# Cumulated gate columns taken at the end of the preceding step, rows from four transposes: a gated DeltaNet and sliding-window layer

## The reference

```python
beta = jax.nn.sigmoid(b)
g = -jnp.exp(a_log) * jax.nn.softplus(a + dt_bias)      # one value for each frame and head
G = jnp.cumsum(gc, axis=-1)                             # gc: g cut into chunks
decay = jnp.exp(jnp.where(causal, G[..., :, None] - G[..., None, :], -jnp.inf))
...
attn_intra = jnp.einsum('bhnid,bhnjd->bhnij', qc, kc) * decay
q_exp = qc * jnp.exp(G)[..., None]
k_tail = kc * jnp.exp(G[..., -1:] - G)[..., None]
g_last = jnp.exp(G[..., -1])
```

## Time and profile before

| what | value |
|---|---|
| median of 3 runs | 2282.87 us (2281.79 to 2283.89) |
| the profiled execution, its own time | 2285.99 us |
| its span in the trace | 2284.2 us |
| mean granted TensorE clock | 0.994 of full speed |
| TensorE busy | 2164.4 us, 95% of the span |
| VectorE busy | 1672.4 us, 73% |
| ScalarE busy | 782.7 us, 34% |
| GpSimd busy | 652.4 us, 29% |

### The profile page before, as it was taken

The page is one execution under the profiler, slowest core; times in us unless marked ns, Lnnn a source line. Parts: engine busy times, 40 slices in busy tenths (PEclk is TensorE's granted clock), DMA queues, the critical chain, the costliest instruction groups (busy, mean ns, idle before and its releaser), DMA issues.

```text
span 2284.2 us, 61174 instructions
## 1 busy us (share of the span) xinstructions
PE 2164.4 (95%) x25926; PEld 1858.0 (81%) x25926; DVE 1672.4 (73%) x4495; ACT 782.7 (34%) x2008; POOL 652.4 (29%) x875
## 2 busy tenths in 40 slices
PE   0389999999999999999999999999999999999996
PEld 0388888888888888888888888888888888888874
DVE  5887777777777777777777777777777777777764
ACT  0533333333333333333333333333333333333332
POOL 0022323322323332232333223233323233322322
PEclk9999999999999999999999999999999999999998
DMA  7100000000000000000000000000000000000000
GB/s 297 53 21 31 2 30 30 31 31 31 30 2 31 31 30 30 31 22 10 31 31 30 31 31 10 23 30 31 30 31 30 2 30 31 30 31 30 21 2 28
DMA packets 26321, 75.19 MB, mean 33 GB/s; under 512 B 5129, under 2 KB 9538, under 8 KB 25026
## 3 DMA queue, kind: packets, MB, share of 16 engines
q1 hardware_dynamic: 26050, 71.29, 8.9%
HBM read 54.50 MB, written 16.78 MB: 31 GB/s over the span
## 4 chain that ended last, share of the span: by engine, by line
PE 92%; DVE 4%; DMA 1%; ACT 1%; issue 0%; SPq 0%; POOLq 0%; POOL 0%; DVEq 0%; ACTq 0%
PE bank L402 37%; PE bank L594 14%; PE bank L409 11%; PE bank L417 9%; PE bank L432 4%; PE bank L452 3%; PE bank L436 2%; PE bank L562 1%; PE bank L528 1%; DVE w_raw L1204 1%; PE bank L549 1%; PE bank L380 1%; PE bank L471 1%; PE bank L440 1%; PE bank L457 1%; PE bank L444 1%
## 5 line engine op out<-in xcount | busy, mean ns | idle before, releaser
L402 PE MATMUL bank<-xt_half,w_raw 128*128 128x128 f16 x15360 | 933.6, 220 | 54.8 <-DVE w_raw L1204 54.3
L402 PEld LDWEIGHTS bank<-xt_half,w_raw 128*128 128x128 f16 x15360 | 896.4, 98 | 62.3 <-DVE w_raw L1204 54.5
L867 DVE SCALAR_TENSOR_TENSOR qkv<-conv_in,cols,qkv 128x128 f32<-128x128 f32 x1152 | 431.3, 416 | 3.5
L409 PE MATMUL bank<-w_raw,xt_half 128*128 128x264 f16 (+1 forms) x1536 | 283.0, 328 | 0.0
L1261 POOL TENSOR_TENSOR cw<-mt,small 128x256 f32<-128x256 f32 x160 | 114.7, 725 | 394.4 <-PE bank L432 373.3
L409 PEld LDWEIGHTS bank<-w_raw,xt_half 128*128 128x128 f16 x1536 | 147.9, 98 | 77.7 <-issue 5.3
L694 ACT ACTIVATE work<-bank 128x256 f32<-128x256 f32 x160 | 61.3, 383 | 397.8 <-PE bank L436 397.8
L594 PE MATMUL bank<-w_o,inv_t 128*128 128x512 f16 x768 | 171.0, 379 | 2.1 <-DVE inv_t L1140 2.1
L594 PE MATMUL bank<-w_o,out_b_half 128*128 128x512 f16 x768 | 171.0, 379 | 0.0
L659 ACT ACTIVATE tanh_c<-qkv 128x512 f32<-128x512 f32 x96 | 60.5, 630 | 270.2 <-DVE qkv L867 270.2
L594 PEld LDWEIGHTS bank<-w_o,inv_t 128*128 128x128 f16 x768 | 73.8, 98 | 85.5 <-DVE inv_t L1140 2.4
(11 more groups left out here) (219 smaller groups left out, 3765.6 us busy)
## 6 DMA issues: line engine op xcount, KB each, us to landing
x_in<-in_x_dram SPq DMA_DIRECT2D x32, 512.0 KB, 4.3
y_out<-in_x_dram SPq DMA_DIRECT2D x32, 512.0 KB, 4.0
out_dram<-y_out SPq DMA_DIRECT2D x32, 512.0 KB, 2.9
w_raw<-in_w_in_dram SPq DMA_DIRECT2D x8, 1024.0 KB, 12.2
w_o<-in_w_out_dram SPq DMA_DIRECT2D x8, 512.0 KB, 12.7
w_raw<-in_w_in_dram SPq DMA_DIRECT2D x8, 384.0 KB, 11.3
w_raw<-in_w_in_dram SPq DMA_DIRECT2D x8, 256.0 KB, 12.1
rot_tab<-in_rotary_dram SPq DMA_DIRECT2D x32, 64.0 KB, 3.9
```

Of the source, the lines that this page charges most:

```text
L402: last = mm(dst[:, 128 * b:128 * b + 128], w_half[:, c, ws, col:col + 128], xt_half[:, xs, c, :], start=(c == 0 and ws + xs == 0), stop=(c ...
L409: last = mm(dst[:, 0:n_col], xt_half[:, xs, c, :], w_half[:, c, ws, col:col + n_col], start=(c == 0 and ws + xs == 0), stop=(c == NC - 1 a ...
L867: last = v.scalar_tensor_tensor(dst, conv_in[:, b, i:i + TOK], tap, dst, ALU.mult, ALU.add)
```

## The change

TensorE gets a new function, `gate_columns`: one product of `upper` with `g_tok` (four columns) into bank 2. It is called at the end of the step in which `g_tok` was formed, between the transposes L608 and `fill(2)`, and waits for `g_ready` of tile t and `state_ready` of tile m. In step 0 it follows the last fill. The product L475 at the start of the step goes. The four row products L471 at the start of the step are replaced by four transposes of `g_cols`, broadcast, and these wait for `g_cols_used`. The wait for `out_a_ready`, which stood ahead of L475, stands ahead of the transposes of Q in place of `g_cols_used`.

VectorE copies the columns after `copy_xt` and ahead of the convolution of Q, instead of at the start of the next step. That copy waits for `g_col_t` and `exp_cols_ready`. At the start of the step the last column of the rows is still copied, now signalling `g_last_ready`.

```diff
+                def gate_columns():
+                    done(pe, g_ready, t)
+                    done(pe, state_ready, m)
+                    mm(bank[2][:, 0:4], upper, g_tok, start=True, stop=True).then_inc(g_col_t, 1)
+
                 if not mix:
                     fill(len(PIECES))
+                    gate_columns()
                     if prep:
                         turn_x(t + 1)
                     return
 
-                done(pe, g_ready, m)
-                done(pe, state_ready, m - 1)
+                done(pe, g_cols_used, m)
                 for h in range(4):
-                    last = mm(bank[2][:, 128 * h:128 * h + 128], g_tok[:, h:h + 1].broadcast_to([128, 128]),
-                              upper, start=True, stop=True)
+                    last = nc.tensor.transpose(heads(2)[:, h, :], g_cols[:, h:h + 1].broadcast_to([128, 128]), ident)
                 last.then_inc(g_row_t, 1)
-                done(pe, out_a_ready, m - 1)
-                mm(bank[3][:, 0:4], upper, g_tok, start=True, stop=True).then_inc(g_col_t, 1)
...
-                done(pe, g_cols_used, m)
+                done(pe, out_a_ready, m - 1)
                 for h in range(4):
                     last = nc.tensor.transpose(heads(3)[:, h, :], q4[:, h, :], ident)
...
                 last.then_inc(o_turned, 1)
+                if proj:
+                    gate_columns()
                 fill(2)
...
                     done(dve, g_row_t, m)
-                    done(dve, exp_cols_ready, m - 1)
-                    v.tensor_copy(g_cols[:, 8:12], heads(2)[:, :, TOK - 1])
-                    done(dve, g_col_t, m)
-                    v.tensor_copy(g_cols[:, 0:4], bank[3][:, 0:4]).then_inc(g_cols_used, 1)
-                    done(dve, g_cols_used, m)
+                    v.tensor_copy(g_cols[:, 8:12], heads(2)[:, :, TOK - 1]).then_inc(g_last_ready, 1)
+                    done(dve, g_last_ready, m)
                     v.tensor_tensor(g_cols[:, 4:8], g_cols[:, 8:12], g_cols[:, 0:4], ALU.subtract)
...
                 if prep:
                     copy_xt(t + 1, True)
                 if proj:
+                    done(dve, g_col_t, t)
+                    done(dve, exp_cols_ready, m)
+                    v.tensor_copy(g_cols[:, 0:4], bank[2][:, 0:4]).then_inc(g_cols_used, 1)
                     convolve(t, FILL_Q, range(4), qs_ready if mix else None, m)
```

More of the change, by code:

```diff
@@ L222, in build @@
             sem(n) for n in ("gram_t", "k_turned", "v_turned", "q_turned", "sq_ready"))
-        norm_link, k_norms_ready, norms_ready, key_norm_ready, m_ready, at_ready, vn_ready, k_tail_ready = (
-            sem(n) for n in ("norm_link", "k_norms_ready", "norms_ready", "key_norm_ready", "m_ready", "at_ready",
+        norm_link, g_last_ready, k_norms_ready, norms_ready, key_norm_ready, m_ready, at_ready, vn_ready, k_tail_ready = (
+            sem(n) for n in ("norm_link", "g_last_ready", "k_norms_ready", "norms_ready", "key_norm_ready", "m_ready", "at_ready",
                              "vn_ready", "k_tail_ready"))
```

## The result

The changed kernel takes 2268.44 us (median of 4 runs, 2267.31 to 2269.20), the kernel before 2283.38 us in the same comparison (median of 4, 2281.79 to 2285.98). The ratio is 0.9931, with a 95% interval of 0.9915 to 0.9946: faster by 0.7%, 14.9 us. The forecast was 15.6 us and 2267.3 us.

What follows compares the result with a forecast made beforehand. The prediction took gapless TensorE to bound the steady steps. It summed 13.4 us there, 2.3 in step 1 and -0.1 in the last step to 15.6 us, giving 2267.3 us, with an 8-in-10 range of 2263 to 2273 us.

Steps and rivals of the forecast that it cites:

- What bounds the kernel: Steady steps: TensorE is busy throughout at full clock, so work leaving its queue leaves the time if other engines keep up.
- Rows: Step's start: four transposes at 0.44 us replace products at 0.89 us, gaining 0.45 us a step, bounds 0.40 and 0.49.
- The column product: Moved between L608 and L402 at about the same cost: net 0, bounds -0.05 and +0.10 us a step.
- steady sum: Steps 2 to 31: thirty times 0.445 us gives 13.4 us gained, bounds 11.1 and 14.7.
- Slack: Gram products L417 behind the output's scaling (`y_used`): 0.16 us left of 0.80, with least favourable bounds 0.
- Rival A: Gram products wait for `y_used`, which takes the saving's place: 2270.6 to 2280.8 us, put at 2272; chance 0.14.
- Ends: First and last steps: 2.3 us gained and 0.1 us lost, with +-1.5 us for half-clock stretches in the last.
- step 1: First step: the wait at L495 goes and the fill behind starts earlier, gaining 2.3 us, bounds 0.5 and 2.8.
- last step's start: Saving swallowed by L417's wait for L1154; moved L475 delays the chain by 0.12 us.
- B: Ends go otherwise: a half-clock stretch more or first-step gain missing, 2269 to 2271 us; one less, 2265 to 2266; chance 0.10.
- C: Transposes in a row drop the clock to half at each step's start: 36 us slower in thirty, 2303 us; chance 0.02.
- D: Transposes of the broadcast column take two instructions like products, so only the first step gains: 2280.7 us; chance 0.02.

Runs made afterwards that it cites:

- transposes twice: Changed kernel with each of the four row transposes issued twice: 2283.38 us, ratio to the kernel before 0.9994.
- rows as products: Changed kernel with the four row transposes undone to products of the gate with the triangle: 2281.62 us, ratio to the kernel before 0.9991.
- before, conv. late: Kernel before with one unread VectorE reduction (0.60 us) added ahead of the convolution of Q: 2286.38 us, ratio 1.0005.
- changed, conv. late: Changed kernel with one unread VectorE reduction (0.60 us) added ahead of the convolution of Q: 2285.40 us, ratio to the kernel before 0.9990.
- copy first: Changed kernel with the copy of the columns ahead of the turned input's copy: 2267.81 us, ratio to the kernel before 0.9930.
- columns first: Changed kernel with the column product ahead of the transposes L611 (old L608): 2269.73 us, ratio to the kernel before 0.9941.
- transposes alone: Kernel before with rows from four transposes, columns still formed and copied at the step's start: 2285.88 us, ratio 1.0009.

## Why the prediction was right

*What bounds the kernel.* Right. TensorE had no gap before and has none after, and the same 0.44 us once more (the transposes twice) are found in full in the period.

*Rows.* Forecast 0.44 us for the four transposes and 0.45 us of gain; measured 0.44 us in the chain, and 0.45 us of gain by the run that undoes only this (13.6 us in thirty steps). Two instructions became one of the same length.

*The column product.* Forecast net 0, with -0.05 to +0.10. Measured: 0.12 us at its new place, 0.02 us on the fill behind it, and 0.05 us less on the transposes of K. A gain of 0.03 to 0.04 us a step, inside the bounds I had named and not taken. Thirty steps gained 14.8 us, where the forecast had 13.4 (bounds 11.1 and 14.7). The steady sum is the term that was mis-sized, by 1.4 us, mostly through this. Its bounds were also too narrow for its own terms: a gain of 0.40 to 0.49 us from the rows and a cost of -0.05 to +0.10 us from the column product make 0.30 to 0.54 us a step, 9.0 to 16.2 us in thirty, and only that range holds the 14.8.

*Slack.* Forecast 0.16 us left of 0.80, measured 0.09 by the timeline and 0.12 by the added reduction. TensorE's part before it had become 0.63 us shorter instead of 0.57, the chain 0.08 longer (10.15 us from the turned input to the signal against 10.07). Rival A was real in kind and did not come about for want of a tenth of a us; with 0.60 us of other work it took the whole gain.

*Ends.* The stages by the trace, in us: the columns are from the second half of L380 in step 0 to the first output projection; from there thirty steps and the first half of one more output projection (5.18 us); from there to the waiting L417 of the last step; and the rest of the span. With the columns first, the column product (0.14 us) lies in the second stage instead of the third.

| kernel | step 1 | thirty steps | last step's start | rest |
|---|---|---|---|---|
| before | 63.40 | 2018.58 | 13.14 | 56.80 |
| changed | 61.14 | 2003.78 | 13.29 | 55.73 |
| rows as products | 61.15 | 2017.37 | 13.28 | 60.52 |
| transposes twice | 61.14 | 2016.79 | 13.27 | 56.92 |
| before, conv. late | 62.37 | 2018.58 | 13.14 | 60.53 |
| changed, conv. late | 61.87 | 2018.33 | 13.28 | 58.79 |
| copy first | 61.17 | 2003.78 | 13.28 | 56.82 |
| columns first | 61.17 | 2004.91 | 13.18 | 55.77 |
| transposes alone | 68.72 | 2014.98 | 13.62 | 54.90 |

Step 1 gained 2.26 us (2.3 forecast) in this pair of executions, and by the mechanism that was forecast. This is the L380 from which the 63.40 us before are counted:

```profile
132.28 0.62 PE L380 MATMUL bank<-masks,shared 128*128 128x128 f16 x8 [0.69 <-DVE shared L826]
```

VectorE's line from L380 to the end of its product L1005 (now L1007) takes 22.97 us before and 22.96 after. The fill that needs this product started 25.36 us behind L380 before, 2.4 us late, and 23.11 us after. In all five kernels that form the columns early and add nothing ahead of VectorE's convolution this fill starts 23.11 to 23.13 us behind L380, though TensorE reaches the Gram products anywhere from 13.03 to 14.01 us. That is why step 1 takes 61.14 to 61.17 us in all five, and why products, double transposes and the earlier copy changed nothing there.

But the size of this gain was in part luck. Before the change the 48 matmuls behind the wait at L495 took 4.03 us, at a mean clock of 0.68. The prediction had them run at the full clock once that idle time was gone. In the kernel before with the added reduction the idle time is longer (2.87 us), and the clock was full all the same:

```profile
148.95 2.84 PE L402 MATMUL bank<-xt_half,w_raw 128*128 128x128 f16 x48
```

Its step 1 took 62.37 us, with more work on VectorE. Against such an execution of the kernel before, the gain of step 1 would have been 1.2 us at most. What decides which of the two comes is not shown by any run.

The last step's start lost 0.15 us (0.12 forecast). The rest is the same program in all, but took 54.9 to 60.5 us. It goes with the granted clock there; these are the busy times of that stage in the run with the rows as products and in the one with the transposes alone:

```profile
2223.80:2284.30 60.50, 40.80 (x248) 29.69 (x248) 25.43 (x57) 12.29 (x34) 14.20 (x15) 0.79 0.07 27
```

```profile
2230.30:2285.20 54.90, 35.13 (x248) 25.45 (x248) 25.46 (x57) 12.36 (x34) 14.20 (x15) 0.90 0.08 29
```

The same 248 matmuls took 40.8 us of TensorE at a mean clock of 0.79 and 35.1 us at 0.90. The forecast gave the ends +-1.5 us. That was too narrow for the last stage of a single execution (5.6 us between these), and it is the reason why the spans of two executions tell 18.7 us and the medians 14.9: 14.8 in thirty steps and 2.3 in step 1, less 0.15, are 16.9, and the setup (0.7 us) and the last stage (1.1 us) came on top in these two executions. That the medians show 2 us less than 16.9 is within their scatter (before 2281.8 to 2286.0 us). The scatter goes with the clock: of the 46 further runs of the kernel before, the nine with a mean clock of 0.997 took 2281.5 to 2283.3 us and the eight with 0.993 took 2289.4 to 2290.2. From 165 to 2195 us the clock is 1.00 in every trace, so it is the ends that scatter. How the ends of the untraced runs divide is not known, so this last part stays argued. That 14.9 us were measured where 15.6 were forecast is therefore partly luck: the steady steps gained 1.4 us more than forecast, and the medians do not show all of it.

*Rivals.* A: excluded for the changed kernel (no wait), and shown to begin 0.1 us further on. B: the ends do go otherwise from one execution to the next, the last stage in all kernels and step 1 in the kernel before. C: excluded by the clock of 1.00. D: excluded by the count of 128.

## What to carry to other kernels

Where one engine has no gap, price a change by the chain of work and by the period of a step, not by the median: 0.04 us a step was plain in the period, and invisible in whole runs. Then compute how much slack the engine's own saving uses up at the next place that waits for another engine. Here 0.49 us of gain used 0.71 of 0.80 us of slack, and the next saving of the same kind on TensorE ahead of the Gram products will be lost unless the chain through convolution, tanh and squares is shortened first. A replacement that needs another engine's copy pays only if that copy is off the path: with the columns formed a step earlier the whole change saved 0.49 us, at the step's start 0.12 us. And where another engine's line sets a step's end, as VectorE's does in step 1, neither more nor less work on TensorE changes it.

## What was not expected of the hardware

The last stage runs the same work in 54.9 to 60.5 us, as the granted clock changes between its two levels (1.2 and 2.4 GHz) in a stage where TensorE waits for others again and again, up to 3.4 us at a time. Two executions can differ by over 5 us there, more than a third of what this change gains, whatever the kernel. And a wait on the critical path can show in the matmuls' list of waits with little more than half its length: 0.27 us a step where the period had grown by 0.48 us. The weight loads' list had 0.45 us.
